# Attention phase of a two-layer decoder: two queue orders changed, the third weight part's stores against the next gate rows' loads on SyncE, and the second part's rounding against the tanh on ScalarE

## The reference, cut to what matters

```python
def _mixer_layer(x, p, pos, k_buf, v_buf, s0, w_in, sinks, attn_g, lb, hg_g, w_out, ln_g, ln_b, w_pp, w_pg):
    z = jnp.einsum('btd,dc->btc', x, w_in)
    q, k, v, g_attn, hq, hf, hi, g_hg = jnp.split(z, _split_points(), axis=-1)
    ...
    attn = _rmsnorm(attn, attn_g) * jax.nn.silu(g_attn)
    ...
    mix = jnp.einsum('btc,cd->btd', jnp.concatenate([attn, o_hg], axis=-1), w_out)
    h = _layernorm(DN_ALPHA * x + mix, ln_g, ln_b)
    gate = jax.nn.sigmoid(jnp.einsum('btd,de->bte', h, w_pg))
    y = h + gate * jnp.einsum('btp,pd->btd', p, w_pp)
```

## Time and profile before

| | us |
|---|---|
| median of 3 runs (lowest, highest) | 2553.34 (2550.48, 2555.16) |
| the profiled execution | 2549.0 |
| its span, first to last instruction | 2547.2 |
| TensorE matmul busy in the span | 2496.2 (98%) |
| VectorE, ScalarE, GpSimd busy | 1704.5 (67%), 1112.1 (44%), 1168.7 (46%) |
| data moved | 365.44 MB, 143 GB/s on the mean |

### The profile page before, as it was taken

The page is one execution under the profiler, slowest core; times in us unless marked ns, Lnnn a source line. Parts: engine busy times, 40 slices in busy tenths (PEclk is TensorE's granted clock), DMA queues, the critical chain, the costliest instruction groups (busy, mean ns, idle before and its releaser), DMA issues. The chain is left out here.

```text
span 2547.2 us, 55195 instructions
## 1 busy us (share of the span) xinstructions
PE 2496.2 (98%) x20706; PEld 2047.9 (80%) x20706; DVE 1704.5 (67%) x3230; ACT 1112.1 (44%) x2542; POOL 1168.7 (46%) x1119
## 2 busy tenths in 40 slices
PE   8999989999999999999999999899999999999998
PEld 6788868888888788878878888688888887887887
DVE  5777777777776676654557777777777776766343
ACT  4455465555555510133334454555555554102322
POOL 2234315555556611487412343165555556115863
PEclk9999999999999999999999999999999999999999
DMA  5455552011110488765734555610111104887532
GB/s 182 162 172 185 179 189 66 27 43 43 47 34 25 175 284 296 273 200 188 250 121 166 187 172 172 206 35 31 43 43 43 39 33 178 317 275 262 172 135 91
DMA packets 176099, 365.44 MB, mean 143 GB/s; under 512 B 19104, under 2 KB 98464, under 8 KB 170272
## 3 DMA queue, kind: packets, MB, share of 16 engines
q1 hardware_dynamic: 175504, 363.11, 41.5%
q10 hardware_dynamic: 432, 0.08, 0.0%
HBM read 227.14 MB, written 137.89 MB: 143 GB/s over the span
## 5 line engine op out<-in xcount | busy, mean ns | idle before, releaser
L1942 PE MATMUL r_Z<-w_rec_parts,w_rec_xh 128*128 128x512 f32 x1920 | 610.6, 399 | 1.8 <-DVE r_kT L1763 0.9
L1942 PEld LDWEIGHTS r_Z<-w_rec_parts,w_rec_xh 128*128 128x128 f32 x1920 | 348.1, 188 | 72.0 <-issue 3.6
L1942 PE MATMUL r_Z<-w_rec_parts,w_rec_xl 128*128 128x512 f32 x960 | 376.1, 392 | 0.0
L124 PE MATMUL a_Z<-w_attn_high,w_attn_xh 128*128 128x512 f32 (+1 forms) x816 | 302.8, 371 | 12.0 <-DVE w_attn_low L211 9.7
L124 PE MATMUL a_Z<-w_attn_low,w_attn_xh 128*128 128x512 f32 (+1 forms) x816 | 291.0, 357 | 0.0
L124 PE MATMUL a_Z<-w_attn_high,w_attn_xl 128*128 128x512 f32 (+1 forms) x816 | 290.9, 356 | 0.0
L1644 ACT ACTIVATE r_E<-r_E 128x512 f32<-128x512 f32 x230 | 145.4, 632 | 295.9 <-DVE r_E L1800 293.5
L1535 POOL TENSOR_TENSOR r_qE<-r_qT,r_E 128x256 f32<-128x256 f32 x230 | 183.8, 799 | 193.7 <-ACT r_E L1644 127.5
L1942 PEld LDWEIGHTS r_Z<-w_rec_parts,w_rec_xl 128*128 128x128 f32 x960 | 180.2, 188 | 39.3
L1535 POOL TENSOR_TENSOR r_kE<-r_kT,r_E 128x256 f32<-128x256 f32 x230 | 200.0, 870 | 0.0
L124 PEld LDWEIGHTS a_Z<-w_attn_high,w_attn_xh 128*128 128x128 f32 x816 | 155.1, 190 | 40.4 <-issue 20.2
(11 more groups left out here) (340 smaller groups left out, 6413.0 us busy)
## 6 DMA issues: line engine op xcount, KB each, us to landing
dram_h_rows<-o_hb SPq DMA_DIRECT2D x34, 512.0 KB, 3.8
o_raw<-dram_hT SPq DMA_DIRECT2D x34, 512.0 KB, 4.3
o_hb<-dram_h_rows SPq DMA_DIRECT2D x34, 512.0 KB, 3.9
dram_y_all<-o_hb SPq DMA_DIRECT2D x34, 512.0 KB, 4.0
w_attn_xraw<-dram_xT SPq DMA_DIRECT2D x33, 512.0 KB, 5.1
w_rec_slot<-dram_w_in SPq DMA_DIRECT2D x16, 1024.0 KB, 8.5
o_mraw<-dram_mixT SPq DMA_DIRECT2D x32, 512.0 KB, 5.6
dram_hT<-o_hT SPq DMA_DIRECT2D x128, 128.0 KB, 2.6
```

The lines of the kernel that those rows point to most:

```text
L124: mm = pe.matmul(out, a[:, c, :], b[:, c, :], start=(first and c == chunks[0] and a is xh and b is wh), stop=(last and c == chunks[-1] and ...
L1942: mm = pe.matmul(banks[what], x[:, c, :], w[:, cols[what]], start=(c == 0 and x is xh[k] and w is wh[c]), stop=(c == KC - 1 and x is xl[k]))
```

## The change

On SyncE, in `exchange_part` of a third part, the wait for the third sum and the two loads of the next gate rows move from ahead of the wait for the part's remainder and its two stores to behind them. On ScalarE, in `rest`, the rounding of the second part moves from behind the tanh of the gate to ahead of it. Nothing else is changed; no instruction is added or removed.

```diff
             def exchange_part(c):

                 t, which = (c - KC) // 4, (c - KC) % 4
-                if c >= KC and which == 2 and t < 3:
-                    sp.wait_ge(*part_in[2].at(16 * (c // 4) + 16))
-                    load_gate(t + 1)
                 sp.wait_ge(*S["w_split"].at(KC + c + 1))
                 ...
                     sp.dma_start(to, of).then_inc(S["part_st"].sem, 16)
+                if c >= KC and which == 2 and t < 3:
+                    sp.wait_ge(*part_in[2].at(16 * (c // 4) + 16))
+                    load_gate(t + 1)
                 load_part(c + 4)
...
             def rest(j, k, c=None):
                 exps(j, k)
                 copy_v(j + k, 1 - k)
-                gate_tanh(j + k, 1 - k)
                 if c is not None:
                     high_part(*c)
+                gate_tanh(j + k, 1 - k)
                 copy_attnT(j, k)
                 move_v(j + k, 1 - k)
```

## The result

| | before | after |
|---|---|---|
| median of the runs compared (lowest, highest), us | 2551.54 (2549.88, 2556.22), 9 runs | 2562.16 (2555.09, 2565.99), 9 runs |
| ratio to before, 95% interval | | 1.0032 [1.0021, 1.0042] |
| the profiled execution, its span, us | 2549.0, 2547.2 | 2555.09, 2553.3 |
| fourteen steps of layer 0, of layer 1, us | 271.28, 270.19 | 273.60, 274.69 |
| the two stretches together, us | 541.47 | 548.29 |

The kernel became slower by 0.3%, 5.4 to 10.7 us by the interval. The prediction had +2.8 us and put most of its weight on "within 0.2%"; what came is the rival "the rows are late, and the kernel is slower". The 2562.16 also lies above the range's high end of 2560.8.

The account below looks back on a forecast made before the run. TensorE, busy throughout, was taken to bound the kernel, VectorE barely ahead. Late rows lose 3 x 0.45 + 3 x 0.86 = 3.93 us, less 1.09 regained: +2.8, median 2553.34 + 2.8 = 2556.1 us; range 2551.2 to 2560.8.

Parts of the forecast that it names:

- the rows are late, and the kernel is slower: Rival: gate rows landing from about 7.7 us after the first store lose over 5.1 us, from 8.2 +8.7; chance 0.25.
- what bounds the kernel: TensorE, busy throughout at 19.30 us a step, with VectorE only 0.2 to 0.4 us ahead of it.
- the chain of the loss: Late rows delay GpSimd's sums, root and `split_low`, which holds VectorE's `nmax`: 0.45 us a step in layer 0, 0.86 in layer 1.
- VectorE's small lead: VectorE's unfolding ends 0.2 to 0.4 us ahead of TensorE's values; what delays its chain by more is paid in full.
- the rounding: On ScalarE, the second part's 1.14 us rounding fits the 3.20 us wait ahead of the tanh, which starts as before.
- layer 0's 1.09 us: Layer 0's excess over layer 1 in fourteen steps, claimed regained when the earlier remainder avoids GpSimd's fourth sum; gain 0 to 1.09.
- the landing, 7.3 us: Gate rows loaded behind the stores land 7.3 us after the first store's issue, with 6.3 and 8.7 as the ends.
- The x load: Moved behind the gate rows on SyncE, landing 8.7 us after the first store at the latest; costed at nothing.
- The release from landing to first sum: GpSimd's first sum starts 0.25 us after the rows land, as from the rounding's end to the remainder's start.
- The free time ahead of the values: Part of `nmax`'s delay that costs TensorE nothing: 0.24 plus 0.09 us in layer 0, 0.09 in layer 1.
- My upper bound of the landing: Rows landing 8.7 us after the first store: losses of 1.53 and 1.75 us a step, sum +8.7.

## Why the prediction was wrong

**Right: what bounds the kernel, and the chain of the loss.** VectorE's small lead, the rows, the sums that wait for them, the root and `split_low` behind them, and `nmax` held in `split_low`: each step is in the rows of after, and the kernel with `split_low` behind the rotation shows that the last one carries all of it. The Trainium skill's "SBUF — State Buffer", section "Who interferes with whom", has a VectorE instruction with two SBUF inputs and a GpSimd instruction that reads SBUF hold a shared port pair as an exclusive lock, so that the later one is blocked to the end. The trace agrees: 1.51 to 1.83 us for `nmax`, a 0.16 us operation, in the six long steps, and 2.37 for `sinkd` in the kernel with three more sums.

**Right: the rounding.** The tanh costs nothing and layer 0's 1.09 us comes back; the kernel with that half alone has 1.08. It comes back because the remainder ends earlier, ahead of TensorE's row sum, and not because every long remainder goes: three are left in the change. Right as well: no step without gate rows lost anything.

**Wrong: the landing, 7.3 us, the term on which the sum hung.** Measured are 7.87, 8.56, 8.26, 8.11, 8.52 and 8.33, on the mean 8.28 after the first store. I had taken 7.3 as "nearer to the row with the same stores", the x load at 6.3. But that row is one load, and the sums wait for the second of two; what I put on top for the second, 1.0 us, came from no row. What a second load adds stood in the trace of before, in rows that I did not use. These are landings there: the two gate-row loads as they stand before, behind the four small stores of `mixT` (issued at 268.01 and 268.65), a 512 KB load issued at 284.82 behind stores whose first was issued at 283.97, and two loads, a part of W_out and x (issued at 118.25 and 119.09), behind stores whose first was issued at 117.41.

```profile
w_attn_kc<-dram_w_gate SPq DMA_DIRECT2D x1, 512.0 KB, 3.9
w_attn_vc<-dram_w_gate SPq DMA_DIRECT2D x1, 512.0 KB, 4.6
...
a_part<-dram_w_gate SPq DMA_DIRECT2D x1, 512.0 KB, 6.3
...
w_attn_kcT<-dram_w_out SPq DMA_DIRECT2D x1, 512.0 KB, 5.8
w_attn_xraw<-dram_xT SPq DMA_DIRECT2D x1, 512.0 KB, 6.2
```

The first two land at 271.9 and 273.2: the second 1.3 behind the first. The third lands 7.1 after the first store. So the rows bounded the second gate load at 6.3 + 1.3 = 7.6 to 7.1 + 1.3 = 8.4, and not at 6.3 to 8.7 with a choice near the lower end. The middle, 8.0, lies behind 7.7, from which my own text had the kernel slower by over 0.2%. The last two rows are a second pair of loads behind a pair of stores: I had called the one of layer 1, at 8.7, the only one. Here the second load lands 7.9 after the first store, 1.3 behind the first, and the two pairs have the measured 8.28 in their middle. The first gate load itself landed at 6.57 to 7.21, 6.9 on the mean, later than the 5.92 to 6.37 of x in the same place, and the second 1.4 behind it. Of the miss of 1.0 us, then, some 0.6 is the first load being slower than x, and 0.4 the second adding 1.4 where I had 1.0.

What slows the first one is open, so the larger part of the miss has a size but no cause. With one load behind it, it took 6.63 to 6.99, with two 6.57 to 7.26, which would fit that loads share the queue; but the load at 284.82, of other blocks of W_gate, landed at 7.1 with none issued behind it in the next 7 us. The x load, which I had put at 8.7 after the first store at the latest, landed at 9.1 to 9.8; no wait for it shows.

**Smaller terms.** The release from landing to first sum was 0.06 to 0.07, not 0.25. The free time ahead of the values was 0.36 in layer 0 and 0.12 in layer 1 (delay of `sinkd` less loss of the step), near the 0.33 and 0.09 that I had. With 8.28 and 0.06 my working gives first sums at 280.99 and 1545.24, losses of about 1.24 and 1.75 a step, and a sum of +7.9; the stretches show +6.8. So with the landing right the working gives slower by over 0.2%, 1.1 us from what the stretches show.

**The range.** My upper bound of the landing gave +8.7, 2562.0 on the median I started from, and I cut the range at 2560.8 with a chance of 0.25 on that side. The rows above would have had the late rows as the likeliest case.

**Open.** The interval is 5.4 to 10.7 us, and the stretches explain 6.8. Whether a us or two more is lost elsewhere cannot be told: the parts of the program that the change does not touch vary by more than that between executions.

## What to carry to other kernels

When a load moves behind other transfers, ask for the landing of the last one that its consumer waits for: look for every place in the trace with the same number of transfers ahead, and take each load as a term of its own, instead of one row that resembles it. Then follow the waiting engine's in-order tail to the end, since the cost may sit in an instruction that has nothing to do with the transfer; here it was the remainder of x, pushed onto a 128x4 operation of VectorE. If such a push cannot be avoided, move the long instruction to where the other engine has no operation with two SBUF inputs: that took away the whole loss here without making a transfer earlier.

## What the runs showed of the hardware

A 128x4 operation of 0.16 us took 1.51 to 1.83 us in the six long steps, where a GpSimd instruction of 2.4 us had begun 0.6 to 0.9 us ahead of it, and 2.29 to 2.44 in the kernel with three more sums, where the two began within 0.15 us of each other: the delay goes by what is left of the other instruction and not by the size of the own. Two stores of 512 KB landed 2.8 and 4.8 us after the first was issued, and the loads behind them at 6.9 and 8.3 on the mean, the third (x) at 9.5: from the first load on, one more 512 KB load comes every 1.2 to 1.7 us. And the loads' landing reached a waiting GpSimd instruction within 0.07 us, much less than the 0.25 us that I had borrowed from a release between two engines.
